# A two-layer diffusion backbone: pool and attention projections as three passes over split weights, and another order in the last down projection

## The reference, cut to what matters

```
y = (g[:, :, 0] * (attn_out @ w_oa)
     + g[:, :, 1] * (pooled @ w_ob)
     + g[:, :, 2] * (fourier @ w_oc))
return y @ w_out
...
out = out + combine[..., e:e + 1] * ((silu(h @ w1[e]) * (h @ w3[e])) @ w2[e])
```

## Time and profile before

| | us |
|---|---|
| median of 3 runs | 1874.2 |
| the profiled execution | 1875.7 |
| its span | 1873.9 |
| TensorE busy | 1844.4 |
| VectorE busy | 768.9 |
| ScalarE busy | 460.8 |
| direct products L2074, busy | 131.6 |
| low parts L1137, 79 units | 183.3 |

### The profile page before, as it was taken

The page is one execution under the profiler, slowest core; times in us unless marked ns, Lnnn a source line. Parts: engine busy times, 40 slices in busy tenths (PEclk is TensorE's granted clock), DMA queues, the critical chain, the costliest instruction groups (busy, mean ns, idle before and its releaser), DMA issues.

```text
span 1873.9 us, 29603 instructions
## 1 busy us (share of the span) xinstructions
PE 1844.4 (98%) x12622; PEld 1128.2 (60%) x12622; DVE 768.9 (41%) x1292; ACT 460.8 (25%) x751; POOL 100.0 (5%) x127
## 2 busy tenths in 40 slices
PE   8999999999999999999999999999999999999997
PEld 5776666667788888887788993333333333333334
DVE  3783443478667646546555551020202020202022
ACT  4433233322522222224444331100000000000001
POOL 0160000010001001100400000000000000000000
PEclk9999999999999999999999999999999999999997
DMA  9422212255246546632343488999999999999980
GB/s 378 141 87 90 79 46 102 90 180 190 91 158 201 191 146 233 235 113 76 116 147 113 157 319 342 398 359 400 363 404 364 397 361 405 369 396 361 405 333 24
DMA packets 75154, 438.54 MB, mean 234 GB/s; under 512 B 9488, under 2 KB 10256, under 8 KB 45200
## 3 DMA queue, kind: packets, MB, share of 16 engines
q1 hardware_dynamic: 63360, 393.65, 55.1%
q0 software_dynamic: 11664, 43.00, 6.9%
HBM read 435.57 MB, written 1.05 MB: 233 GB/s over the span
## 4 chain that ended last, share of the span: by engine, by line
PE 93%; DVE 3%; ACT 2%; issue 1%; DMA 1%; SPq 0%; ACTq 0%; DVEq 0%
PE ps L2258 24%; PE ps L1803 12%; PE ps L1805 12%; PE ps L1804 12%; PE ps L2276 8%; PE ps L2074 7%; PE ps L2280 4%; PE ps L2023 2%; PE ps L1980 2%; PE ps L2049 1%; PE ps L2034 1%; DVE wlo L1137 1%; PE ps L1988 1%; PE ps L2002 1%; PE ps L2221 1%
## 5 line engine op out<-in xcount | busy, mean ns | idle before, releaser
L2258 PE MATMUL ps<-estage,xg 128*32 128x448 f32 (+1 forms) x4608 | 459.1, 557 | 0.0
L1803 PE MATMUL ps<-h_hi,whi 128*128 128x512 f32 (+1 forms) x960 | 368.9, 384 | 10.2 <-DVE wlo L1137 3.9
L1805 PE MATMUL ps<-h_hi,wlo 128*128 128x512 f32 (+1 forms) x960 | 344.4, 359 | 0.0
L1804 PE MATMUL ps<-h_lo,whi 128*128 128x512 f32 (+1 forms) x960 | 344.1, 358 | 0.0
L2258 PEld LDWEIGHTS ps<-estage,xg 128*32 128x32 f32 x4608 | 148.8, 110 | 302.1 <-issue 301.1
L1650 DVE TENSOR_TENSOR eu<-et,ps 128x224 f32<-128x224 f32 (+1 forms) x72 | 24.4, 395 | 514.1 <-ACT et L1067 514.1
L1137 DVE TENSOR_TENSOR wlo<-stage,whi 128x2048 fp32r<-128x2048 f32 x79 | 183.3, 2320 | 84.2 <-ACT whi L752 84.2
L1803 PEld LDWEIGHTS ps<-h_hi,whi 128*128 128x128 f32 x960 | 181.1, 189 | 54.1 <-issue 13.8
L1804 PEld LDWEIGHTS ps<-h_lo,whi 128*128 128x128 f32 x960 | 181.3, 189 | 35.9 <-issue 10.5
L1805 PEld LDWEIGHTS ps<-h_hi,wlo 128*128 128x128 f32 x960 | 181.1, 189 | 27.2
L752 ACT ACTIVATE whi<-stage 128x2048 fp32r<-128x2048 f32 x79 | 150.9, 1910 | 163.8 <-PE ps L1805 163.7
(11 more groups left out here) (244 smaller groups left out, 1750.5 us busy)
## 6 DMA issues: line engine op xcount, KB each, us to landing
estage<-in_moe SPq DMA_DIRECT2D x152, 1024.0 KB, 7.4
estage<-in_moe SPq DMA_DIRECT2D x128, 896.0 KB, 6.3
stage<-in_split SPq DMA_DIRECT2D x79, 1024.0 KB, 5.1
gw<-in_mods POOLq DMA_DIRECT2D x80, 512.0 KB, 3.9
dw<-in_direct SPq DMA_DIRECT2D x36, 512.0 KB, 3.8
mw_a<-in_early SPq DMA_DIRECT2D x8, 512.0 KB, 8.2
mw_b<-in_early SPq DMA_DIRECT2D x8, 512.0 KB, 15.8
xT<-in_x SPq DMA_DIRECT2D x4, 512.0 KB, 5.6
```

Source lines behind the costliest of these rows:

```text
L1803: pe.matmul(out, hi, rhs_hi, start=first, stop=False)
L1804: pe.matmul(out, hi, rhs_lo, start=False, stop=False)
L1805: ins = pe.matmul(out, lo, rhs_hi, start=False, stop=last)
L2258: ins = pe.matmul(up_bank(x, c, t)[q * TOK:(q + 1) * TOK, 0:n], xg[:, x % 2, kk, t * TOK:(t + 1) * TOK], rows[:, q * n:(q + 1) * n], start ...
```

## The change

- The projections of pool and attention (16 of 24 products a layer) move from the direct stream to the split stream, right behind their gate tile, and run as three passes. The Fourier products stay direct, two a load.
- ScalarE writes the pooled rows as a high part (`pool_hi`), VectorE a low part (`pool_low`, in `part`); attention's rows get a high part (`attention_hi`, in `part`) and a low part (`attention_low`). TensorE's waits for pooled rows become waits for the low part (`br_lo`).
- The landing buffers go from three to two; `LANDING` and `FREED` follow.
- The last down group runs the upper columns of all its four units first (`last_down`); VectorE's copies and adds of them come ahead of the wait for the rest (`last_part_rows`), and the scatter waits for the first low part alone before its first two steps.
- Three semaphores are merged into others; `split_hi`, `split_lo` and where they are called are as before.

```diff
-LANDING = (7, 8, 9, 10, 11, 12, 13, 0, 1, 2, 3, 4, 5, 6)
-FREED = (7, 3, 4)
+LANDING = (6, 7, 8, 9, 10, 11, 12, 13, 0, 1, 2, 3, 4, 5)
+FREED = (8, 2, 4)
...
-DENSE_STAGE = 3
+DENSE_STAGE = 2
...
-        tiles += [(("gate", layer, m), KD) for m in range(KD * BRANCHES)]
+        for m in range(KD * BRANCHES):
+            tiles.append((("gate", layer, m), KD))
+            if MERGE[m][1] != 2:
+                tiles.append((("proj", layer, m), KB))
...
-        out += [("pool", layer), ("v", layer), ("head", layer, 0)]
-        for h in range(HEADS):
-            if h % 2 == 1 and h + 1 < HEADS:
-                out.append(("head", layer, (h + 1) // 2))
-            out.append(("proj", layer, h))
-        out += [("proj", layer, n) for n in range(HEADS, NM // 2)]
+        out += [("pool", layer), ("v", layer)]
+        for n in range(HEADS // 2):
+            out += [("head", layer, n), ("proj", layer, n)]
...
+            if m % 4 == 0 and m < BESIDE:
+                add(("d", direct_at[("proj", layer, m // 4)]))
             if m % 4 == 2 and m < 2 * (HEADS - 1):
                 add(("d", direct_at[("head", layer, m // 4 + 1)]))
-            add(("d", direct_at[("proj", layer, m // 2)]))
+            if MERGE[m][1] != 2:
+                tile("proj", layer, m)
...
+    def product_of(layer, m):
+
+        if MERGE[m][1] == 2:
+            return S("o_full"), earlier("o_full", layer) + m // 2 + 1
+        return S("walked"), walk.tile("proj", layer, m)
...
-                act.activation(br[:, 1, g, lc:T], pool_bank(g)[:, 0:T - lc], ACT.Copy,
+                act.activation(pool_hi[:, g, lc:T], pool_bank(g)[:, 0:T - lc], ACT.Copy,
...
+            def attention_hi(k):
+
+                act.wait_ge(S("br_a"), earlier("br_a", layer) + 4 * (k + 1))
+                if k == 0:
+                    act.wait_ge(S("walked"), walk.tile("proj", layer, BESIDE - 2))
+                act.activation(part[:, k, lc:T], br[:, 0, k, lc:T], ACT.Copy).then_inc(S("attn_hi"), 1)
...
+                if n == len(todo):
+                    for k in range(KB - 1):
+                        attention_hi(k)
...
+            def pool_low(g):
+
+                dve.wait_ge(S("br_b"), earlier("br_b", layer) + g + 1)
+                dve.scalar_tensor_tensor(part[:, g, lc:T], pool_bank(g)[:, 0:T - lc], s_pool[:, layer, g:g + 1], pool_hi[:, g, lc:T],
+                                         ALU.mult, ALU.subtract).then_inc(S("br_lo"), 1)
...
+            def attention_low(k):
+
+                dve.wait_ge(S("attn_hi"), earlier("attn_hi", layer) + k + 1)
+                dve.tensor_tensor(attn_lo[:, k, lc:T], br[:, 0, k, lc:T], part[:, k, lc:T], ALU.subtract).then_inc(S("attn_lo"), 1)
...
+        def last_part_rows(p, done, count):
+
+            def copied(n, b, q):
+
+                dve.tensor_copy(y_d[n * TOK:(n + 1) * TOK, :], ps[b][q * TOK:(q + 1) * TOK, :]).then_inc(done, 1)
+
+            dve.wait_ge(S("y_upper"), p)
+            copied(1, 4, 0)
+            copied(2, 4, 3)
+            for n in (1, 2):
+                rows = slice(n * TOK, (n + 1) * TOK)
+                dve.wait_ge(done, count + n)
+                dve.tensor_tensor(y_d[rows, :], y_d[rows, :], ps[4][rows, :], ALU.add).then_inc(done, 1)
+            dve.wait_ge(S("e_used"), last_used(p - 1))
+            copied(0, 3, 3)
...
-                slot = direct_unit(("proj", layer, m // 2))
                 if m == 0:
-                    pe.wait_ge(S("br_b"), earlier("br_b", layer) + GROUPS)
+                    pe.wait_ge(S("br_lo"), earlier("br_lo", layer) + GROUPS)
                 else:
                     pe.wait_ge(S("o_used"), earlier("o_used", layer) + m)
-                if m == BESIDE:
-                    pe.wait_ge(S("br_a"), earlier("br_a", layer) + 2 * HEADS)
+                if b == 2:
+                    slot = direct_unit(("proj", layer, m // 4))
+                    for k in range(KB):
+                        ins = pe.matmul(ps[1][:, 0:T - lc], dw[:, slot, 4 * (m // 2 % 2) + k, :], br[:, b, k, lc:T], start=(k == 0), stop=(k == KB - 1))
+                    ins.then_inc(S("o_full"), 1)
+                    return
+                hi, lo = (part, attn_lo) if b == 0 else (pool_hi, part)
                 for k in range(KB):
-                    ins = pe.matmul(ps[1][:, 0:T - lc], dw[:, slot, 4 * (m % 2) + k, :], br[:, b, k, lc:T], start=(k == 0), stop=(k == KB - 1))
-                ins.then_inc(S("o_full"), 1)
+                    if m == BESIDE:
+                        pe.wait_ge(S("attn_lo"), earlier("attn_lo", layer) + k + 1)
+                    block_passes(ps[1][:, 0:T - lc], ("proj", layer, m), k, hi[:, k, lc:T], lo[:, k, lc:T], k == 0, k == KB - 1)
...
+            def last_down(d):
+
+                units = len(DOWNS[d]) // 2
+                blocks = [DOWNS[d][2 * u:2 * u + 2] for u in range(units)]
+                for u in range(units):
+                    rows = landed(0, LAST_DOWN + u)
+                    for q in range(QUADS):
+                        t, i = 1 + q // 2, q % 2
+                        ins = pe.matmul(ps[4][q * TOK:(q + 1) * TOK, :], turned(*blocks[u][i], t), rows[:, i * D + 512:i * D + D],
+                                        start=False, stop=(u == units - 1))
+                ins.then_inc(S("y_upper"), 1)
+                for u in range(units):
+                    rows = landed(0, LAST_DOWN + u)
+                    for i, (c, b) in enumerate(blocks[u]):
+                        for q in range(QUADS):
+                            t, f = (q, 0) if q < TILES_E else (0, 1)
+                            ins = pe.matmul(ps[3][q * TOK:(q + 1) * TOK, :], turned(c, b, t), rows[:, i * D + f * 512:i * D + f * 512 + 512],
+                                            start=False, stop=(u == units - 1 and i == 1))
                     ins.then_inc(used, 1)
...
-            pe.wait_ge(S(f"{tag}_lo"), 2 * n + 2)
             for k4 in range(KD // 2):
+                if k4 % 2 == 0:
+                    pe.wait_ge(S(f"{tag}_lo"), 2 * n + k4 // 2 + 1)
```

More of the change, by code:

```diff
@@ L273 @@
     "t_full": _ITEMS, "pT": _ITEMS, "pv": _ITEMS, "br_a": 2 * HEADS,
-    "gate": KD * BRANCHES, "o_full": KD * BRANCHES, "o_used": KD * BRANCHES, "y_add": 2 * KD,
+    "gate": KD * BRANCHES, "o_full": KD, "br_lo": GROUPS, "attn_hi": KB, "attn_lo": KB, "o_used": KD * BRANCHES, "y_add": 2 * KD,
     "y_hi": KD, "y_lo": KD, "x_mix": KD,
@@ L432, in build @@
     fg = Region(free).take("fg", [P, 2, 2 * SEQ])
+    pool_hi = Region(br_at + KB * T * 4).take("pool_hi", [P, KB, T], F32R)
+    attn_lo = Region(br_at).take("attn_lo", [P, KB, T], F32R)
+    part = nc.alloc_sbuf_tensor_at("part", [P, KB, T], F32R, offset=(end - KB * T * 4) // 64 * 64)
     pkv = mixer.take("pkv", [P, KKV, T])
@@ L458, in build @@
     hf = nr.take("hf", [P, KD, SEQ])
-    sq_between = Region(h_lo_at + 2 * LINE).take("sq_between", [P, 3, T])
+    sq_between = Region(h_lo_at + 18 * LINE).take("sq_between", [P, 3, T])
     sq_fin = Region(phase).take("sq_fin", [P, KD, SEQ])
@@ L712, in _ @@
                 for t, a in tables[1:4]:
-                    load_small(t, a).then_inc(S("tables_again"), 16)
+                    load_small(t, a).then_inc(S("tables"), 16)
             if kind == "d":
@@ L976, in merged_hi @@
                 act.activation(ym_hi[:, j, lc:T], yacc[:, j, lc:T], ACT.Copy, scale=0.5).then_inc(S("y_hi"), 1)
+            attention_hi(KB - 1)
             for m in range(BESIDE, NM):
@@ L1360, in _ @@
                 dve.tensor_tensor(rows[:, :, 1:HALF], rows[:, :, 1:HALF], both[:, :, EVEN:SEQ], ALU.subtract).then_inc(S("br_c"), 1)
+            pool_low(2)
+            pool_low(3)
             todo = items(layer)
@@ L1407, in merge @@
                 j, b = MERGE[m]
-                dve.wait_ge(S("o_full"), earlier("o_full", layer) + m + 1)
+                dve.wait_ge(*product_of(layer, m))
                 dve.wait_ge(S("gate"), earlier("gate", layer) + m + 1)
@@ L1433, in _ @@
             dve.memset(kT[32:64, 1, :], 0.0).then_inc(S("zeros"), 1)
+            def attention_low(k):
+                dve.wait_ge(S("attn_hi"), earlier("attn_hi", layer) + k + 1)
+                dve.tensor_tensor(attn_lo[:, k, lc:T], br[:, 0, k, lc:T], part[:, k, lc:T], ALU.subtract).then_inc(S("attn_lo"), 1)
             for n in range(len(todo) + 3):
+                if n == len(todo) + 1:
+                    for k in range(KB - 1):
+                        attention_low(k)
                 if n >= 3 and (n - 3) % per == per - 1:
@@ L1455, in merged_lo @@
                     .then_inc(S("y_lo"), 1)
+            attention_low(KB - 1)
             if layer == 1:
@@ L1663, in expert @@
                             combine()
-                            dve.sem_inc(S("comb"), 1)
+                            dve.sem_inc(S("routed"), 1)
                         if c == 0 and x == 0:
@@ L1764, in _ @@
                     if layer == 1:
-                        pool.wait_ge(S("tables_again"), 16 * 3)
```

(19 more changed lines are left out.)

13 lines of the change are left out of this document (8 added, 5 removed).

## The result

The changed kernel takes 1929.24 us (median of 4 runs, 1923.10 to 1931.66), the kernel before 1874.20 (1873.84 to 1874.57). The ratio is 1.0284 [1.0259, 1.0308]. The forecast was 1912 with a range up to 1926: the direction and the stalls are right, the size is 17 us short, and the time is outside the range. The same kernel taken a second time (e10) had a median of 1924.49, just inside the range, so some 5 us of the miss may be chance, and 12 stay. The profiled execution took 1931.66, its span is 1929.9, 56.0 more than before.

The account below looks back on a forecast made before the run. TensorE, busy 98% of 1873.9 us, bounds the kernel. Profiled 1875.7 + 48.4 + 5.9 + 0.5 + 5.0 - 15.6 - 6.0 = 1913.9, less 1.5 for the median: 1912.4 us, range 1894 to 1926.

Parts of the forecast that it names:

- The look-ahead and the stalls: Both layers' mixers: VectorE makes units' low parts after the preceding merge, so TensorE waits 23 times, 48.4 us.
- U3: Split unit, counted from the first gate, starting at product 4; stall 0.15 us in layer 0, 2.3 in layer 1.
- U12: Split unit starting at product 18, after attention; stall 2.1 us in layer 0, 0.4 in layer 1.
- U16: Split unit starting at the first output tile; stall 5.1 us in layer 0, 4.1 in layer 1.
- Pool's load: Pool's direct load stands behind the third gate unit: 5.4 us late in layer 1, 0.5 in layer 0.
- Landing buffers: Unit loads with two buffers: 0, hidden by TensorE's work; without that cover some 10 us.
- The tail: Last down group, scatter and squares: scatter 3.0 us earlier, squares partly at upper clock, 6.0 us gained (3.0 to 8.5).
- The products: Pool and attention products as three passes: 11.0 us gained in layer 0, 4.6 in layer 1, together 15.6.
- The clock in the new gaps: Nine new TensorE gaps of 3.3 us or more: three falls to the lower clock taken, 5 us (0 to 15).
- Rival C: The clock falls at each long gap and loads come late too: 1922 to 1932; chance 0.18.
- Rivals A: Only stalls with no TensorE work in between (16.2 us) and the pool's load (5.9) appear: 1875; chance 0.08.
- B: Low parts are in time at every unit's first block, so none of the 48.4 us is paid: 1858.5; chance 0.06.

Follow-up runs that it names:

- e10: The changed kernel run once more, unchanged, as base for the run with half-length fillers; 1924.49 us, ratio 1.0269 to the kernel before.
- e7: The changed kernel with low parts made early everywhere and the pool's load issued ahead of the third gate unit; 1855.95 us, ratio 0.9895.
- e1: The changed kernel with VectorE making the next unit's low part ahead of the item's row maximum and ahead of merge(m); 1865.82 us, ratio 0.9941.
- e2: The changed kernel with pool, value and first head loads issued ahead of the third gate unit, not behind it; 1923.06 us, ratio 1.0243.
- e3: The kernel before with two landing buffers instead of three and the expert-weight slots that follow; 1873.93 us, ratio 0.9993.
- e4: The kernel before with only the change's last down group and tail; 1869.17 us, ratio 0.9959.
- e5: The changed kernel with warming matmuls, twice too long, in four gaps (ahead of gate 20 and the output tiles, both layers); 1928.17 us, ratio 1.0289.
- e9: The changed kernel with warming matmuls of about the gap's length in four gaps (ahead of gate 20 and output tiles, both layers); 1919.31 us, ratio 1.0233.
- e6: The changed kernel with the low part moved ahead of merge(m) only after attention, steps 16 to 23; 1895.53 us, ratio 1.0111.
- e8: The kernel with early low parts and early pool load, with 52 instead of 30 warming matmuls at the start; 1859.83 us, ratio 0.9918.

## Why the prediction was wrong by its size

Landmarks of the profiles, us later (+) or earlier (-) than in the kernel before:

```
                      changed    e10     e7
first split pass L0     +4.7    -1.4   -1.3
first score L0          +7.3    -0.7   -1.3
last score L0           +7.3    -0.6   -6.7
output tiles L0        +17.6    +9.7   -6.4
first split pass L1    +16.8    +9.2   -7.8
first score L1         +24.5   +16.7   -7.0
last score L1          +47.7   +40.2   -9.2
output tiles L1        +60.3   +52.7  -10.3
experts                +62.7   +55.1  -10.3
scatter                +60.0   +52.5  -13.5
squares                +58.4   +50.9  -15.0
```

**The look-ahead and the stalls** (forecast 48.4 us, 23 of them): right, nearly one by one (U3 and U8 of layer 0, 0.15 each, did not appear). Layer 1's, forecast then measured: U1 3.4, 3.28; U3 2.3, 2.33; U4 3.8, 3.71; U6 3.4, 3.28; U8 2.3, 2.33; U9 3.4, 3.27; U11 1.85, 1.48; U12 0.4, 0.40; U13 3.3, 3.27; U14 1.85, 1.76; U15 0.4, 0.40; U16 4.1, 4.05. Layer 0's are 3.8 beside attention (forecast 4.8) and 11.9 after it (13.1); its U16 waited 5.19 for a forecast of 5.1. Together 45.3, 3 less than forecast. The largest single miss is U12 of layer 0, 1.05 for 2.1. e1 shows the cause, by moving nothing else.

**Pool's load** (5.9): layer 1's wait is 5.5 and is gone in e2. Layer 0's half microsecond shows as a wait of 0.48 before its pool matmuls in e10 (1.14 in the first profile), for which the profile names no releaser, and is gone in e2 too. **Landing buffers** (0): 0, shown by e3 for the kernel before. **The tail** (6.0): 6.7 to 6.9, from this profile and e4. The squares' clock did fall, at 1920 instead of ahead of them.

**The products** (15.6 gained): supported, not measured apart. Beside attention the gain is 5.4 in layer 0 (e7 and e1) for 5.5 forecast, and 2.2 in layer 1 for 2.3. After attention it is less plain: layer 0 is 0.3 us longer in e7 for 5.5 gained by forecast; it waits 2.7 us anew there and has 1.7 of clock cost, and 1.4 stays open (1.5 in e1). Layer 1 is 1.2 shorter for 2.3, with a new wait of 0.3, and 0.9 stays open. Between the ratios of e4, which has the tail alone, and e7 lie some 12 us.

**The clock in the new gaps** (three falls, 5 us): this step failed. I took three falls of nine since "here work at full rate stands on both sides". Work on both sides protected nothing: nine of nine gaps had a fall, in both profiles of the changed kernel, at 17.1 and 18.8 us by half of the stretches. With the gap filled at four places there was no fall behind it (e5, e9). The Trainium skill ("TensorE: Matmul & The Clock Gate", section "Why this matters for your kernels") holds that idle gaps between bursts throw the clock back. By that all nine would pay, and the trace agrees, with nine of nine. Rival C (1922 to 1932) was the better forecast, but only half of it came true: the clock fell at each long gap, which by itself gave 1922, while the late loads that were to bring the rest did not come. What brought the first median to 1929 was the start. The row I reasoned from was the tail's, which had one gap of the same size and a fall. That made one of one, and I discounted it.

**The start** (no term of its own): also missed. In the first profile 17.1 us of the first 55 ran at the lower level and the first score came 7.3 us late; in e10's profile of the same kernel it was 0 us and 0.7 early. e4's late start shows that no change of the schedule is needed for it. The three narrow runs of the kernel before (0.7 us apart) hid it from me: over more runs that kernel itself spans 1872 to 1880. This makes the first median partly chance: 1929.24 there, 1924.49 in e10. That the second lies inside the range does not save the step on the clock, whose nine falls stand in both profiles.

The sum, from three spans. "Waits" are all rows of TensorE's waits view, added (22.9 us before). The clock is half of the time at the lower level ahead of the tail (10.2 us before), and of the tail's gain the 3.8 that are not the wait of 2.9. The products' row is the forecast in every column, not a measurement:

```
            forecast   changed          e10              e7
waits        +51.8     74.9: +52.0      74.2: +51.3      24.9: +2.0
products     -15.6          -15.6            -15.6            -15.6
clock         +5.0     51.2: +20.5      37.5: +13.7       6.8: -1.7
tail's clock  -3.0           -3.8             -3.8             -3.8
sum          +38.2          +53.1            +45.6            -19.1
span         +38.2          +56.0            +48.5            -18.2
```

The forecast of the waits (48.4 + 5.9 + 0.5 - 3.0) is right within 1 us; nearly all of the miss is the clock. In the changed kernel its 15.5 us too much are 12.1 at the new gaps and 6.8 at the start, less 3.4 at the norms; in e10 the 8.7 too much are 13.8 at the gaps, less 1.7 at the start and 3.4 at the norms. 0.9 to 2.9 us stay open in each column; the products' 2.3 that do not show after attention may be a part of it. Rivals A (1875) and B (1858.5) fall by the 25 waits. B's mechanism, the low parts in time with the pool's load still late, is what e1 builds: 1865.8 us, 7 above B's sum, with 17.1 us at the lower level at the start of its profile. e7 has the pool's load early too; without its 5.9, B's sum would be 1852.6, and e7 takes 1855.95.

## What to carry to other kernels

When a producer's step stands behind other work in an engine's written order, count how many units of consumer work lie between it and its need for each unit of the new stream, not for the mean: a change that makes work cheaper but units more frequent can use up that lead, and moving the producing step in its queue gives it back (e1: 1866 us where the changed kernel takes 1924 to 1929). Price a gap of TensorE such as those of 3.3 us here as the gap plus the work behind it at half the clock, 1.7 us each and sometimes 3.4. Take the scatter of the start into the range: a few runs that agree within 1 us don't show that it is absent.

## What the runs showed of the hardware that was not expected

- In seven profiles (both of the changed kernel, e1, e2, e5, e6, e9) there were 42 gaps of 3.27 us or more between layer 0's first scores and layer 1's experts, and 41 of them had a stretch at the lower level at their end. The exception is U1 in e9, 3.27 us. The twelve gaps of 2.33 us had none. Length alone doesn't settle it: in e9 a gap of 1.75 us was followed by one, in e7 one of 1.96 us, and in e8 one of 2.25 us.
- The first passes behind a gap can still run at full rate. Layer 1's U6 in the changed kernel (timeline of TensorE): 0.12 us from pass to pass, then 0.21.

```profile
1042.25 0.28 PE L1863 MATMUL ps<-h_lo,whi 128*128 128x256 f32 x1
1042.37 0.28 PE L1864 MATMUL ps<-h_hi,wlo 128*128 128x256 f32 x1
1042.49 0.35 PE L1862 MATMUL ps<-h_hi,whi 128*128 128x256 f32 x1
1042.64 0.41 PE L1863 MATMUL ps<-h_lo,whi 128*128 128x256 f32 x1
1042.85 0.41 PE L1864 MATMUL ps<-h_hi,wlo 128*128 128x256 f32 x1
```

- Equal starts differ from execution to execution. Of the first 55 us the changed kernel had 17.1 us at the lower level in one profile and 0 in the other; the kernel before had 3.4, and e4, with the same start, 13.7. What decides it is open; e8's longer filler didn't remove it.
- The two norm stages fell in the kernel before (483 and 855 us) but in the changed kernel's profiles not at all, and in e7 and e4 one of the two did. Their price, 1.7 us each by half of the stretch, came and went between the profiles without a change there.
